# Routing stage: who multiplies the found places by their indices, GpSimd or VectorE

## The chip, the cores and the metric

The kernel runs on one core of a Trainium2 chip, alone. The metric is the device time of one execution in microseconds (us), the median of several. Six parts of the core matter here: TensorE (PE, matrix products; PEld is its weight load), VectorE (DVE), ScalarE (ACT), GpSimd (POOL), SyncE (SP, which issues most DMAs) and the DMA engines. They run side by side and wait for each other on semaphores only.

## What is computed

One decoder layer over 528 rows (16 meta tokens and 512 real ones, width 2048): attention and a recurrence side by side, an output projection, and then PEER, a feed-forward layer that picks experts per token. The change lies in PEER's routing:

```python
q = (xt @ w_q).reshape(T, PEER_HEADS, 2, PEER_DHALF)
s = jnp.einsum('thcd,hcnd->thcn', q, sub_keys).astype(jnp.float32)
s1v, s1i = lax.top_k(s[:, :, 0], PEER_TOPK)
s2v, s2i = lax.top_k(s[:, :, 1], PEER_TOPK)
cand = (s1v[..., :, None] + s2v[..., None, :]).reshape(T, PEER_HEADS, PEER_TOPK * PEER_TOPK)
cidx = (s1i[..., :, None] * PEER_NKEYS + s2i[..., None, :]).reshape(T, PEER_HEADS, PEER_TOPK * PEER_TOPK)
top_s, top_pos = lax.top_k(cand, PEER_TOPK)
eidx = jnp.take_along_axis(cidx, top_pos, axis=-1)
gates = jax.nn.softmax(top_s, axis=-1)
```

For each of 8 heads and 512 tokens there are two rows of 128 scores. The 16 best of each are taken with their indices, 16 of the sums of pairs are kept, and the two indices of each kept pair name the expert. The `take_along_axis` is the part that the change touches.

## The kernel before, in words

**Stages.** The layer is a chain of blocks: norm, input projection, attention, recurrence, output projection, norm, routing (`route`, some 1040 to 1290 us of the profiled execution), a table of gates (`gate_table`, to some 1480 us) and the experts (`experts`, to the end at 3562 us). Each engine has its own instruction stream in a block.

**The weights' stream.** The routing projects the normed rows with w_q, one piece of 256 columns for each head m. A piece has four steps g. For each step SP loads a raw tile, ACT rounds it to a high part (L298, `split_high`), and POOL subtracts to get the low part (L312, `split_low`, called a split below). PE takes both parts (L343 to L345, 24 matmuls per step) when the low part is there. There are two buffers of high and low parts, so the split of step g can start only when PE has released step g - 2.

**A head on its way.** After step 0 of piece m, PE makes the scores of head m - 1 (L1423), ACT copies them to SBUF (L1456), and VectorE works on head m - 1. VectorE's head is this list:

- the search over the scores: maxima (L1501), places of the maxima (L1505), removal of them (L1508), and the same again for the next eight
- a cast of the found indices to float (L1528) and the sums of pairs (L1534)
- the same search over the sums
- sixteen numbers per token kept (L1543), bit operations on the places (L1545 to L1548), a cast (L1549), and arithmetic on them (L1550 to L1554)
- `keep` of the head before (two reductions, L1517), which waits for `hot_done`
- two comparisons (L1559, one for each half) that write `route_hot`, a tile of ones and zeros: 4 token blocks x 16 kept pairs x 16 ranks per partition, 1024 elements

**Who multiplies.** `route_hot` is multiplied by the float indices (`route_idx_f`), and the sum over the ranks (`keep`) then is the index of the kept pair. Before, POOL multiplies: `weigh`, two instructions of 128x1024 (L1396). In POOL's stream `weigh(m, s)` stands between the splits of steps 1 and 2 of piece m and works on head m - 2, since it waits until `places_met` has reached m - 1. The last two heads' multiplications stand behind the last split. `route_hot`, `route_idx_f` and the scores have two slots each, for even and odd heads.

**The end of the stage.** Behind head 7 VectorE subtracts the top score (L1579, L1580), ACT takes the exponential, VectorE keeps the last head (L1517) and scales the gates (L1584 to L1586). PE then transposes the picks for the table (L1633).

Of the kernel before, what the change touches and what calls it, by code (L numbers as in the profile page):

```python
# [24 lines left out]
ALU = mybir.AluOpType  # L25
# [7 lines left out]
P = 128  # L33
# [3 lines left out]
TB = T // P  # L37
# [14 lines left out]
PH, NK, TOPK = 8, 128, 16  # L52
# [7 lines left out]
class Count:  # L60
# [10 lines left out]
    def link(self, ins):  # L71

        self.up(ins)
        self.wait()
# [599 lines left out]
def pl(start, count):  # L674
    return bass.ds(start, count)
# [670 lines left out]
def route(nc, place, kb, stream, xT, picks, cst, plain_stored):  # L1346


    with ExitStack() as ctx:
        def sem(name):  # L1350
            return ctx.enter_context(nc.semaphore(f"route_{name}"))
# [6 lines left out]
        hot = place("route_hot", [P, 2, 2, TB, TOPK, TOPK], F32, kb + 20)  # L1358
        val = place("route_val", [P, 2, TB, TOPK], F32, kb + 36)
        idx = place("route_idx", [P, 2, TB, TOPK], U32, kb + 36.5)  # L1360
        idx_f = place("route_idx_f", [P, 2, 2, TB, TOPK], F32, kb + 37)
# [9 lines left out]
        places_met, hot_done, waited = sem("places_met"), sem("hot_done"), sem("waited")  # L1371
# [6 lines left out]
        def each_head(eng, head, peeled):  # L1378

            for m in range(peeled):  # L1380
                head(m, m % 2, True)
            with eng.Fori(peeled // 2, PH // 2) as i:
                for s in range(2):
                    head(i * 2 + s, s, False)

        @block.sync
        def _(sp):
            stream.load_rest(sp, PH)

        @block.gpsimd  # L1390
        def _(pool):
            def weigh(m, s):

                pool.wait_ge(places_met, m - 1)
                for c in range(2):
                    last = pool.tensor_tensor(  # L1396
                        hot[:, s, c], hot[:, s, c],
                        idx_f[:, s, c].unsqueeze(2).to_broadcast([P, TB, TOPK, TOPK]), ALU.mult)
                last.then_inc(hot_done, 1)

            def head(m, s, first):
                for g in range(QSTEPS):
                    if not (first and m == 0 and g < 2):
                        stream.split_low(pool, m, g)
                    if g == 1 and not first:
                        weigh(m, s)

            each_head(pool, head, 2)
            weigh(PH, 0)
            weigh(PH + 1, 1)  # L1410

        @block.tensor
        def _(pe):
# [72 lines left out]
        def _(dve):  # L1486
# [3 lines left out]
            def take_wait():  # L1490

                dve.sem_inc(waited, 1)

            def top16(rows, rests, values, places):

                take_wait()
                for part in range(2):
# [12 lines left out]
                    link(last)  # L1510
                    take_wait()

            def keep(m, s):

                dve.wait_ge(hot_done, m)
                for c in range(2):
                    last = dve.tensor_reduce(picks[c][:, :, pl(m * TOPK - TOPK, TOPK)], hot[:, s, c],  # L1517
                                             AX.X, ALU.add)
                link(last)

            def head(m, s, first):
# [9 lines left out]
                for ranks, width, at in ((slice(0, WIDE), TOPK, 0),  # L1531
                                         (slice(WIDE, TOPK), NARROW, WIDE * TOPK)):
                    rows = ranks.stop - ranks.start
                    last = dve.tensor_tensor(  # L1534
                        cand[:, :, at:at + rows * width].rearrange("p b (i j) -> p b i j", j=width),
                        val[:, 0, :, ranks].unsqueeze(3).to_broadcast([P, TB, rows, width]),
                        val[:, 1, :, 0:width].unsqueeze(2).to_broadcast([P, TB, rows, width]),
                        ALU.add)
# [16 lines left out]
                if not (first and m == 0):  # L1555
                    keep(m, 1 - s)

                for c in range(2):
                    last = dve.tensor_tensor(  # L1559
                        hot[:, s, c].rearrange("p b n r -> p (b n) r"),  # L1560
                        pos_f[:, c].rearrange("p b n -> p (b n)").unsqueeze(2)
                        .to_broadcast([P, TB * TOPK, TOPK]),
                        cst["iota"][:, 0:TOPK].unsqueeze(1).to_broadcast([P, TB * TOPK, TOPK]),
                        ALU.is_equal)
                last.then_inc(places_met, 1)

            dve.wait_ge(plain_stored, 16)
            head(0, 0, True)
            head(1, 1, True)
            with dve.Fori(1, PH // 2) as i:  # L1570
                count.enter(i - 1, 2 * HEAD_LINKS)
                for s in range(2):
                    head(i * 2 + s, s, False)
                count.leave(PH // 2 - 1)
# [5 lines left out]
            dve.tensor_tensor(gates, gates, tops.unsqueeze(3).to_broadcast([P, TB, PH, TOPK]),  # L1580
                              ALU.subtract).then_inc(shifted, 1)
            keep(PH, 1)
            dve.wait_ge(exp_done, 1)
            link(dve.tensor_reduce(total[:, 1], gates, AX.X, ALU.add))  # L1584
# [651 lines left out]
```

## Time and profile before

| | us |
|---|---|
| median of 3 runs | 3577.05 |
| lowest, highest | 3573.82, 3586.83 |
| the profiled execution | 3564.46 |
| its span on the core | 3562.6 |
| PE busy | 3357.4 (94%) |
| DVE busy | 2235.9 (63%) |
| ACT busy | 1118.1 (31%) |
| POOL busy | 1162.3 (33%) |

The profile is of one execution. Its span runs from the first to the last instruction, and some 2 us lie around it. Busy time is a mean over stages with different limits: in the experts, the last two thirds, PE is never idle, while in the routing it has idle time. A row in order of time gives start, length, engine, line, operation and shapes, and in brackets how long the engine had been idle and what ended that. The length of an instruction includes time in which it stood on the engine and could not proceed.

### The profile page before, as it was taken

The numbers are of one execution on the slowest core, as the hardware profiler recorded it, in microseconds if no ns is written. First come the engines' busy times: TensorE is split into PE (matmuls) and PEld (weight loads), VectorE is DVE, ScalarE is ACT, GpSimd is POOL, SyncE is SP. The second block draws the span as 40 slices with busy tenths as digits, with TensorE's granted clock in tenths as the row PEclk, the third lists the DMA queues.
The fourth block names the chain that finished last, engine by engine and source line by source line (L and its number), as shares of the span: only waits on it lengthen the run. The fifth ranks groups of instructions, "written<-read, shape, count | busy, mean of one in ns | idle before, by whom it ended". The sixth has DMA issues, their size and how long they took to land.

```text
span 3562.6 us, 51459 instructions
## 1 busy us (share of the span) xinstructions
PE 3357.4 (94%) x16926; PEld 2941.1 (83%) x16926; DVE 2235.9 (63%) x3877; ACT 1118.1 (31%) x1732; POOL 1162.3 (33%) x870
## 2 busy tenths in 40 slices
PE   7999999777989947899999999999999999999999
PEld 5778876666868746799998998998998998998998
DVE  2003412794027899667777777777777777777676
ACT  3122223443232249332233223232233222222222
POOL 2344431263435510322322322323323333333332
PEclk9999999899999979999999999999999999999999
DMA  4233320003322124887887888887888888888876
GB/s 140 74 86 95 96 80 20 1 1 118 95 105 83 59 83 188 298 265 262 275 263 260 275 261 264 269 267 259 273 265 263 271 265 264 269 266 263 269 263 233
DMA packets 276020, 686.84 MB, mean 193 GB/s; under 512 B 120544, under 2 KB 120800, under 8 KB 273504
## 3 DMA queue, kind: packets, MB, share of 16 engines
q1 hardware_dynamic: 202224, 417.51, 36.2%
q0 software_dynamic: 73728, 268.47, 22.5%
q8 instruction: 37, 0.61, 0.1%
q14 instruction: 31, 0.25, 0.0%
HBM read 655.48 MB, written 30.41 MB: 193 GB/s over the span
## 4 chain that ended last, share of the span: by engine, by line
PE 59%; ACT 2%; issue 1%; DMA 1%; ACTq 0%; DVE 0%; DVEq 0%; SPq 0%
PE exp_a L1864 10%; PE exp_a L1866 10%; PE exp_a L1865 10%; PE exp_o L1885 10%; PE exp_o L1887 10%; PE exp_o L1883 10%; ACT table_gaps L1682 1%; ACT table_stage L1698 1%; DMA gate_table<-table_stage 0%; PE table_b L1642 0%; ACTq L1682 0%; DMA exp_raw<-in_v 0%; ACTq L1698 0%; PE table_t L1633 0%; DVE table_hot L1668 0%
## 5 line engine op out<-in xcount | busy, mean ns | idle before, releaser
L1864 PE MATMUL exp_a<-x_high,exp_uh 128*128 128x384 f32 x2048 | 686.3, 335 | 10.0 <-DVE exp_ul L1948 10.0
L1866 PE MATMUL exp_a<-x_high,exp_ul 128*128 128x384 f32 x2048 | 685.8, 335 | 0.0
L1865 PE MATMUL exp_a<-x_low,exp_uh 128*128 128x384 f32 x2048 | 685.7, 335 | 0.0
L1887 PE MATMUL exp_o<-exp_vh,exp_al 128*128 128x512 f32 x1536 | 598.2, 389 | 0.0
L1885 PE MATMUL exp_o<-exp_vl,exp_ah 128*128 128x512 f32 x1536 | 598.1, 389 | 0.0
L1883 PE MATMUL exp_o<-exp_vh,exp_ah 128*128 128x512 f32 x1536 | 597.5, 389 | 0.0
L1843 POOL DMA_INDIRECT exp_rows<-in_v_rows,exp_now x256 | 326.8, 1277 | 710.1 <-DVE h L1969 658.6
L1843 POOL DMA_INDIRECT exp_rows<-in_u_rows,exp_now x256 | 299.9, 1171 | 732.1 <-DVE exp_rows L1962 687.1
L1913 ACT CAST exp_vh<-exp_raw 128x1024 fp32r<-128x1024 f32 x256 | 260.0, 1050 | 516.5 <-PE exp_o L1887 493.2
L1948 DVE TENSOR_TENSOR exp_vl<-exp_raw,exp_vh 128x1024 fp32r<-128x1024 f32 x256 | 304.6, 1220 | 164.7 <-ACT exp_vh L1913 164.7
L1864 PEld LDWEIGHTS exp_a<-x_high,exp_uh 128*128 128x128 f32 x2048 | 385.6, 188 | 11.7 <-DVE exp_ul L1948 7.3
L1865 PEld LDWEIGHTS exp_a<-x_low,exp_uh 128*128 128x128 f32 x2048 | 385.6, 188 | 1.2
L1866 PEld LDWEIGHTS exp_a<-x_high,exp_ul 128*128 128x128 f32 x2048 | 385.5, 188 | 0.0
L1924 ACT ACTIVATE exp_act<-exp_a 128x384 f32<-128x384 f32 x128 | 63.0, 492 | 962.3 <-PE exp_a L1866 962.3
L1887 PEld LDWEIGHTS exp_o<-exp_vh,exp_al 128*128 128x128 f32 x1536 | 288.3, 188 | 60.0
L1885 PEld LDWEIGHTS exp_o<-exp_vl,exp_ah 128*128 128x128 f32 x1536 | 288.3, 188 | 59.3
L1883 PEld LDWEIGHTS exp_o<-exp_vh,exp_ah 128*128 128x128 f32 x1536 | 288.3, 188 | 59.2
L1948 DVE TENSOR_TENSOR exp_ul<-exp_raw,exp_uh 128x1024 fp32r<-128x1024 f32 x256 | 309.8, 1221 | 41.5 <-ACT exp_uh L1913 31.5
L312 POOL TENSOR_TENSOR w_in_lo<-w_in_raw,w_in_hi 128x1024 fp32r<-128x1024 f32 x88 | 212.9, 2419 | 332.6 <-ACT w_in_hi L298 332.6
L1969 DVE SCALAR_TENSOR_TENSOR h<-exp_rows,exp_weights,h 128x1024 f32<-128x1024 f32 x256 | 316.5, 1277 | 0.0
L1962 DVE SCALAR_TENSOR_TENSOR exp_rows<-exp_rows,sparse_x 128x1024 f32<-128x1024 f32 x256 | 302.4, 1218 | 0.0
L1989 DVE TENSOR_TENSOR exp_act<-exp_act,exp_gates 128x384 f32<-128x384 f32 x128 | 71.9, 562 | 360.3 <-ACT exp_act L1924 360.3
(290 smaller groups left out, 5182.0 us busy)
## 6 DMA issues: line engine op xcount, KB each, us to landing
exp_raw<-in_u SPq DMA_DIRECT2D x256, 512.0 KB, 5.3
exp_raw<-in_v SPq DMA_DIRECT2D x256, 512.0 KB, 4.4
w_in_raw<-in_w_in SPq DMA_DIRECT2D x88, 512.0 KB, 3.6
gate_table<-table_stage SPq DMA_DIRECT2D x6, 4096.0 KB, 11.6
exp_gates<-gate_table SPq DMA_DIRECT2D x128, 192.0 KB, 5.3
w_out_raw<-in_w_out SPq DMA_DIRECT2D x32, 512.0 KB, 3.7
w_q_raw<-in_w_q SPq DMA_DIRECT2D x32, 512.0 KB, 3.9
x_rows<-in_x SPq DMA_DIRECT2D x4, 1024.0 KB, 8.3
```

The lines of the kernel that those rows point to most:

```text
L312: eng.tensor_tensor(self.lo[:, g % 2], self.raw[:, g % RAW], self.hi[:, g % 2].bitcast(F32), ALU.subtract).then_inc(self.low, 1)
L1843: pool.indirect_dma_start(rows[slot][:, :], None, sparse["u" if kind == "dot" else "v"], bass.IndirectOffsetOnAxis(ap=now[:, turn, place_n ...
L1864: pe.matmul(bank, uh[:, b, c, :], xh[:, 0:DENSE_TB, c, :], start=(c == 0), stop=False)
L1865: pe.matmul(bank, uh[:, b, c, :], xl[:, 0:DENSE_TB, c, :], start=False, stop=False)
L1866: last = pe.matmul(bank, ul[:, b, c, :], xh[:, 0:DENSE_TB, c, :], start=False, stop=(c == DC - 1))
L1883: pe.matmul(bank[:, :], ah[:, key, tokens], vh[:, dc % 2, key, :], start=(key == 0), stop=False)
L1885: pe.matmul(bank[:, :], ah[:, key, tokens], vl[:, dc % 2, key, :], start=False, stop=False)
L1887: last = pe.matmul(bank[:, :], al[:, key, tokens], vh[:, dc % 2, key, :], start=False, stop=(key == KEYS_OF_MACRO - 1))
L1913: act.copy(part(uh if split[0] == "u" else vh, *split, half), raw[:, c % RAW_SLOTS, :])\
L1948: dve.tensor_tensor(part(ul if kind == "u" else vl, kind, which, half), raw[:, slot, :], part(uh if kind == "u" else vh, kind, which, half ...
L1962: done = dve.scalar_tensor_tensor(rows[slot][:, :], rows[slot][:, :], 1.0, sparse["x"][:, half, :], ALU.mult, ALU.mult, accum_out=dots[:, ...
L1969: done = dve.scalar_tensor_tensor(sums, rows[slot][:, :], weights[:, pl(pick(m, kind, t), 1)], sums, ALU.mult, ALU.add)
```

## The change

POOL's function `weigh` and its calls go, and its stream in this stage holds the splits alone. VectorE gets a function `weigh(s)` with the same two instructions on the same operands. It is called at the end of each head, behind the two comparisons and a wait for them on `places_met`. The semaphore `hot_done` is raised by VectorE now, one head earlier in order than before, and `keep` still waits for it.

```diff
--- before.py
+++ after.py
@@ -1389,25 +1389,12 @@
 
         @block.gpsimd
         def _(pool):
-            def weigh(m, s):
-
-                pool.wait_ge(places_met, m - 1)
-                for c in range(2):
-                    last = pool.tensor_tensor(
-                        hot[:, s, c], hot[:, s, c],
-                        idx_f[:, s, c].unsqueeze(2).to_broadcast([P, TB, TOPK, TOPK]), ALU.mult)
-                last.then_inc(hot_done, 1)
-
             def head(m, s, first):
                 for g in range(QSTEPS):
                     if not (first and m == 0 and g < 2):
                         stream.split_low(pool, m, g)
-                    if g == 1 and not first:
-                        weigh(m, s)
 
             each_head(pool, head, 2)
-            weigh(PH, 0)
-            weigh(PH + 1, 1)
 
         @block.tensor
         def _(pe):
@@ -1510,6 +1497,14 @@
                     link(last)
                     take_wait()
 
+            def weigh(s):
+
+                for c in range(2):
+                    last = dve.tensor_tensor(
+                        hot[:, s, c], hot[:, s, c],
+                        idx_f[:, s, c].unsqueeze(2).to_broadcast([P, TB, TOPK, TOPK]), ALU.mult)
+                last.then_inc(hot_done, 1)
+
             def keep(m, s):
 
                 dve.wait_ge(hot_done, m)
@@ -1563,6 +1558,8 @@
                         cst["iota"][:, 0:TOPK].unsqueeze(1).to_broadcast([P, TB * TOPK, TOPK]),
                         ALU.is_equal)
                 last.then_inc(places_met, 1)
+                dve.wait_ge(places_met, m + 1)
+                weigh(s)
 
             dve.wait_ge(plain_stored, 16)
             head(0, 0, True)
```

POOL's stream in the routing, the first part of the loop's body. `w_q_lo` is the low part of a step, `route_hot` the tile that is multiplied. Before:

```order
L312 TENSOR_TENSOR w_q_lo<-w_q_raw,w_q_hi 128x1024
L1394 REGISTER_ALU
L1396 TENSOR_TENSOR route_hot<-route_hot,route_idx_f 128x1024 x2
L311 REGISTER_ALU
L312 TENSOR_TENSOR w_q_lo<-w_q_raw,w_q_hi 128x1024
L311 REGISTER_ALU
L312 TENSOR_TENSOR w_q_lo<-w_q_raw,w_q_hi 128x1024
L311 ISA
L312 TENSOR_TENSOR w_q_lo<-w_q_raw,w_q_hi 128x1024
L311 REGISTER_ALU
```

And now:

```order
L312 TENSOR_TENSOR w_q_lo<-w_q_raw,w_q_hi 128x1024
L311 REGISTER_ALU
L312 TENSOR_TENSOR w_q_lo<-w_q_raw,w_q_hi 128x1024
L311 REGISTER_ALU
L312 TENSOR_TENSOR w_q_lo<-w_q_raw,w_q_hi 128x1024
L311 ISA
L312 TENSOR_TENSOR w_q_lo<-w_q_raw,w_q_hi 128x1024
L311 REGISTER_ALU
L312 TENSOR_TENSOR w_q_lo<-w_q_raw,w_q_hi 128x1024
```

The pair of multiplications between the second and third split is gone, and the splits stand in a row.

VectorE's stream, the end of the second head in the loop's body and what stands behind the loop. `picks` are the kept indices. Before:

```order
L1554 TENSOR_TENSOR route_pos_f<-route_pos_f,route_quarterf 128x64
L77 REGISTER_ALU
L1517 ISA
L1517 TENSOR_REDUCE picks_77<-route_hot 128x4x16
L1517 REGISTER_ALU
L1517 TENSOR_REDUCE picks_78<-route_hot 128x4x16
L77 REGISTER_ALU
L1559 TENSOR_TENSOR route_hot<-route_pos_f,c_iota 128x1024 x2
L1570 REGISTER_ALU
L1570 COMPARE_AND_BRANCH
L1579 COPY route_total<-picks_79 128x32
L1580 TENSOR_TENSOR picks_79<-picks_79,route_total 128x512
L1517 TENSOR_REDUCE picks_77<-route_hot 128x4x16
```

And now:

```order
L1512 ISA
L1512 TENSOR_REDUCE picks_77<-route_hot 128x4x16
L1512 REGISTER_ALU
L1512 TENSOR_REDUCE picks_78<-route_hot 128x4x16
L77 REGISTER_ALU
L1554 TENSOR_TENSOR route_hot<-route_pos_f,c_iota 128x1024 x2
L1561 REGISTER_ALU
L1503 TENSOR_TENSOR route_hot<-route_hot,route_idx_f 128x1024 x2
L1567 REGISTER_ALU
L1567 COMPARE_AND_BRANCH
L1576 COPY route_total<-picks_79 128x32
L1577 TENSOR_TENSOR picks_79<-picks_79,route_total 128x512
L1512 TENSOR_REDUCE picks_77<-route_hot 128x4x16
```

Behind the two comparisons there is now a pair of multiplications, ahead of the branch that ends the loop's body, so every head's search starts behind the multiplications of the head before it.

## Rows read from the trace of the kernel before

**Rows 1.** A stretch of the experts: busy us (instructions) of PE, PEld, DVE, ACT, POOL, clock, DMA.
```profile
1500.00:3500.00 2000.00, 2000.00 (x10186) 1828.67 (x10185) 1477.61 (x1824) 577.16 (x727) 631.78 (x546) 1.00 0.81 267
```

**Rows 2.** The waits of 1040 to 1300 us: sum, times, longest.
```profile
DVE route_val L1501 <- ACT route_scores L1456: 39.2, 6, 32.1
...
PE route_q L343 <- POOL w_q_lo L312: 9.1, 6, 3.6
```

**Rows 3.** VectorE in order of time, the stage's end: start, length, idle before.
```profile
1281.13 0.18 DVE L1579 COPY route_total<-picks 128x32 f32<-128x32 f32 x1
1281.35 2.83 DVE L1580 TENSOR_TENSOR picks<-picks,route_total 128x512 f32<-128x512 f32 x1
1286.41 2.35 DVE L1517 TENSOR_REDUCE picks<-route_hot 128x64 f32<-128x1024 f32 x2 [2.23 <-POOL route_hot L1396]
1288.79 0.69 DVE L1584 TENSOR_REDUCE route_total<-picks 128x32 f32<-128x512 f32 x1
```

**Rows 4.** VectorE in order of time, head 6 and the start of head 7.
```profile
1234.48 0.30 DVE L1501 MAX8 route_val<-route_scores 128x8 f32<-128x128 f32 x1 [1.73 <-ACT route_scores L1456]
...
1245.06 0.69 DVE L1534 TENSOR_TENSOR route_cand<-route_val 128x256 f32<-128x256 f32 x2
...
1251.42 0.19 DVE L1545 TENSOR_SCALAR route_pos<-route_pos 128x64 uint32<-128x64 uint32 x1
...
1253.16 2.35 DVE L1517 TENSOR_REDUCE picks<-route_hot 128x1024 f32 x2
1255.54 2.36 DVE L1559 TENSOR_TENSOR route_hot<-route_pos_f,c_iota 128x1024 f32<-128x1024 f32 x2
1257.82 0.29 DVE L1501 MAX8 route_val<-route_scores 128x8 f32<-128x128 f32 x1
```

**Rows 5.** Groups of 1040 to 1300 us: busy, mean ns | idle before, releaser.
```profile
L1396 POOL TENSOR_TENSOR route_hot<-route_hot,route_idx_f 128x1024 f32<-128x1024 f32 x16 | 38.2, 2410 | 51.9 <-DVE route_hot L1559 51.9
L1559 DVE TENSOR_TENSOR route_hot<-route_pos_f,c_iota 128x1024 f32<-128x1024 f32 x16 | 21.4, 1378 | 0.3
...
L1549 DVE CAST route_quarterf<-route_pos 128x256 f32<-128x256 uint32 x8 | 4.5, 559 | 0.3
L1554 DVE TENSOR_TENSOR route_pos_f<-route_pos_f,route_quarterf 128x64 f32<-128x64 f32 x8 | 3.9, 484 | 0.3
L1545 DVE TENSOR_SCALAR route_pos<-route_pos 128x64 uint32<-128x64 uint32 x8 | 3.7, 464 | 0.0
```

**Rows 6.** VectorE and GpSimd in order of time, where both are at work.
```profile
1097.78 2.40 POOL L312 TENSOR_TENSOR w_q_lo<-w_q_raw,w_q_hi 128x1024 fp32r<-128x1024 f32 x1 [3.47 <-ACT w_q_hi L298]
1097.91 2.41 DVE L1549 CAST route_quarterf<-route_pos 128x256 f32<-128x256 uint32 x1
...
1228.01 1.22 DVE L1517 TENSOR_REDUCE picks<-route_hot 128x1024 f32 x1
1228.13 2.40 POOL L312 TENSOR_TENSOR w_q_lo<-w_q_raw,w_q_hi 128x1024 fp32r<-128x1024 f32 x1 [3.47 <-ACT w_q_hi L298]
```

**Rows 7.** GpSimd and VectorE in order of time, the norm before the routing.
```profile
1029.57 3.33 POOL L312 TENSOR_TENSOR w_q_lo<-w_q_raw,w_q_hi 128x1024 fp32r<-128x1024 f32 x1
1030.62 3.37 DVE L206 TENSOR_SCALAR scaled_rows<-h,ffnnorm_stat 128x2048 f32<-128x2048 f32 x1
```

**Rows 8.** VectorE in order of time, its first work in the routing.
```profile
1080.55 1.65 DVE L1501 MAX8 route_val<-route_scores 128x8 f32<-128x128 f32 x8 [32.10 <-ACT route_scores L1456]
```

**Rows 9.** GpSimd in order of time: the four splits of piece 1, first of 2.
```profile
1068.35 2.39 POOL L312 TENSOR_TENSOR w_q_lo<-w_q_raw,w_q_hi 128x1024 fp32r<-128x1024 f32 x1 [3.05 <-ACT w_q_hi L298]
1074.22 2.40 POOL L312 TENSOR_TENSOR w_q_lo<-w_q_raw,w_q_hi 128x1024 fp32r<-128x1024 f32 x1 [3.48 <-ACT w_q_hi L298]
1079.23 2.40 POOL L312 TENSOR_TENSOR w_q_lo<-w_q_raw,w_q_hi 128x1024 fp32r<-128x1024 f32 x1 [2.61 <-ACT w_q_hi L298]
1086.47 2.40 POOL L312 TENSOR_TENSOR w_q_lo<-w_q_raw,w_q_hi 128x1024 fp32r<-128x1024 f32 x1 [4.84 <-ACT w_q_hi L298]
1091.91 2.40 POOL L312 TENSOR_TENSOR w_q_lo<-w_q_raw,w_q_hi 128x1024 fp32r<-128x1024 f32 x1 [3.04 <-ACT w_q_hi L298]
```

## What the change does to the time, predicted

> **What bounds the kernel now.** I read the page's busy times first, then the waits of the routing stage, then VectorE in order of time through it, and then VectorE and GpSimd side by side.
>
> The experts, the last two thirds, are bound by TensorE: in 2000 us it is busy for 2000.00 at a clock of 1.00 [rows 1]. The change doesn't touch them. What it can do is to move the moment at which they begin, and that moment hangs on the routing's last step. The table of gates starts from VectorE's last sums, which begin at 1288.79 [rows 3], and nothing of the table can start earlier, because its transposes need the picks of all heads.
>
> Within the routing two engines take turns as the bound. VectorE begins head 0 at 1080.55 [rows 8]. Until 1288.79 that is 208.24 us, and I split it:
>
> - An undisturbed head is 1257.82 - 1234.48 = 23.34 us [rows 4]. Head 0 has no keep, which is 1255.54 - 1253.16 = 2.38 less: 20.96. Eight heads are 20.96 + 7 x 23.34 = 184.3.
> - The end: 0.22 for L1579, 0.69 for L1580 if it runs alone (L1584 works on as many elements in 0.69), 2.38 for the two L1517: 3.3 [rows 3, 4].
> - Waits for scores: 39.2 in six waits, 32.1 of them ahead of head 0, so 7.1 [rows 2]. These are TensorE's: it waits 9.1 us for late low parts, in front of which GpSimd's multiplications stand.
> - The wait for GpSimd's last multiplications, 2.23, and L1580 held up by them, 2.83 - 0.69 = 2.1 [rows 3].
> - VectorE standing still beside a split. L1549 issued at 1097.91 takes 2.41, just as long as a split that began at 1097.78 [rows 6]; the other seven take 4.5 - 2.4 = 2.1, or 0.3 each. From the groups [rows 5]: 2.1 in L1549, 8 x (464 - 190) ns = 2.2 in L1545, about 2.1 in L1554 at an undisturbed 0.22, and 16 x (1378 - 1220) ns = 2.5 in L1559. Together 8.9.
>
> The sum is 184.3 + 3.3 + 7.1 + 2.2 + 2.1 + 8.9 = 207.9, against 208.2 measured. The account closes, so VectorE is at its limit for 187.6 of 208 us, and any work that is put on it lies on the path.
>
> **What the change takes away.** GpSimd loses 16 instructions, 38.2 us [rows 5]. They weren't on the path as such; what goes is what they caused: the waits for scores (7.1, since VectorE will be the later one, below), the last wait (2.2) and the hold-up of L1580 (2.1). That is 11.4 us.
>
> **What it adds.** VectorE gets 16 instructions on 1024 elements with two SBUF inputs, the form of L1559. A pair of L1559 takes 1257.82 - 1255.54 = 2.28 from its start to the next instruction [rows 4]. The new wait on its own comparison costs the overlap of two instructions, 1.22 - 1.14, and a little for the semaphore: 0.1, an estimate. So 2.4 per head, and a head is 25.74. Undisturbed: 20.96 + 2.4 + 7 x 25.74 + 3.3 = 206.8, or 1.4 less than now. Nothing but that wait is queued behind it: next on VectorE is the search of the next head, which waits with it.
>
> **What is late next.** GpSimd's splits of piece m come at 1068.35, 1074.22, 1079.23 and 1086.47 plus 23.56 x (m - 1), since 1091.91 - 1068.35 = 23.56 is a piece with no multiplication in it [rows 9]. The scores of head m are then ready at 1080.5 + 23.56 m, those of head 7 at 1245.4. VectorE at 25.74 and more per head never waits for them again, and a split that comes a little late costs nothing. But VectorE also loses its step with TensorE: it drifts by over 2 us per head against the splits, and can no longer stay clear of them as head 6 does now, where nothing exceeds its undisturbed length [rows 4].
>
> **The price of meeting a split.** Three things are read from rows. A VectorE instruction that is issued while a split runs waits until it is over (L1549) [rows 6]. A reduction doesn't: L1517 takes 1.22 beside a split of 2.40 [rows 6]. And where both are queued without a pause they alternate: a split issued at 1029.57 lasts 3.33, to 1032.90, because L206 goes first, and the next L206, issued at 1030.62, lasts 3.37 and so gets through only behind it [rows 7]. So a split that comes due within a chain of VectorE's instructions costs VectorE its full length, about 2.35, and one that already runs costs the rest. In a head such chains are L1528 and L1534 (some 0.8 us, at +10.3), L1543 to L1554 (at +16.8 to +18.5), L1559 (at +21.05 to +23.3), and now the multiplications (to +25.7): the last chain doubles [rows 4]. GpSimd's own multiplications met none of them: they started right behind L1559 (all 51.9 us of idle before them end with it [rows 5]) and ran beside the search, which does not stop for GpSimd.
>
> The Trainium skill ("SBUF — State Buffer", section "Who interferes with whom") names the cause: a VectorE instruction with two SBUF inputs shares a read interface with a GpSimd instruction that reads SBUF, and who issues first holds it for the whole instruction. It doesn't say who is next when both are queued. If VectorE kept it through a chain, the second rival below would hold; the rows above show turns.
>
> **The walk.** I step through the heads with these offsets and the splits' times:
>
> | head | starts | stalls | next starts |
> |---|---|---|---|
> | 0 | 1080.55 | 2.4 in L1549 (there before too), 2.3 at the multiplications (split due 1102.8) | 1108.5 |
> | 1 | 1108.5 | 2.3 in L1552 (1126.35), 2.3 at the multiplications (1133.6) | 1138.9 |
> | 2 | 1138.9 | 2.3 in L1554 (1157.15), 2.4 between the multiplications (1162.6) | 1169.3 |
> | 3 | 1169.3 | 2.4 in L1543 (1186.15), 1.6 in L1559 (1192.0), 2.4 between the multiplications (1197.0) | 1201.5 |
> | 4 | 1201.5 | 0.3 in L1528 (1209.7), 0.1 in L1559 (1220.6) | 1227.7 |
> | 5 | 1227.7 | none, the last split is at 1227.8 | 1253.4 |
> | 6, 7 | 1253.4 | none | 1304.9 |
>
> The stalls sum to 20.9. Undisturbed 206.8 + 20.9 = 227.7, against 208.2: **19.4 us later**. One meeting is a matter of 0.05 us, L1554 at 1157.2 in head 2; without it, and with what shifts behind it, I get 17.0. I take the middle, **18 us**.
>
> All of it should arrive at the end: behind the routing comes a table stage whose engines start together, and then a TensorE without a gap [rows 1]. TensorE's clock is not part of the sum, as it idles for tens of us ahead of the table in both.
>
> **The rivals.**
>
> *Turns that fall well, or a VectorE that keeps its port* (stalls as now). Only a split already at work stops VectorE. Then the stalls are about the 8.9 of today: 206.8 + 8.9 - 208.2 = +7.5 us. For it: head 6 of now shows no stall at all [rows 4]. Against it: the turns of [rows 7], and that this head was in step with TensorE, for whose scores it had waited 1.73.
>
> *Every split of the overlap meets a chain.* In heads 0 to 4 some 24 splits pass, and a head could meet 3 rather than 2 of them: 2 to 5 more meetings of 2.35 on top of the walk's 19.4, or +24 to +31 us. A piece that is itself slowed by late splits would prolong the overlap and lead here.
>
> *Not slower.* The multiplications slip between splits, since ScalarE's rounding, ahead of each split, shifts with TensorE, and the chain ends before a split is due. It decides if fewer than one meeting in all is left: 206.8 - 208.2 = -1.4 us, at best. With head 0's stall, which the change doesn't touch, +1. The 11.4 us won pay for the 19.2 of new work (8 x 2.4) only together with the stalls of 8.9. A gain over 0.5% has no row for it.
>
> **How the numbers follow.** The profiled execution took 3564.46, which is 12.6 below the median of the runs shown, and within it the routing's place is read to 0.1 us; the difference is the same on either, so I add it to the median: 3577.05 + 18 = **3595.0**. Chances: the walk (+16 to +21) 0.56, well-fallen turns (+4 to +12) 0.22, more meetings (+24 to +31) 0.14, not slower (-3 to +3) 0.08. What a measurement of this kernel can tell from no change is about 0.5%, or 17.9 us, and my forecast lies on that line: I give half of the walk to either side. Slower by over 0.5%: 0.28 + 0.14 = 0.42, and a little for losses that no row shows, 0.45; faster 0.02; the same 0.53. The range leaves out the not slower and most of the case of more meetings: 3580 to 3602.
>
> **What would show it right or wrong.** In the profile of the changed kernel: 16 multiplications on VectorE at a mean over 1.6 us though the shortest take 1.21; waits of VectorE for scores only ahead of head 0; TensorE's 9.1 us of waits for splits down to some 1; its last product of this stage some 12 us earlier than now; heads 5 to 7 at 25.7 us each; and the last sums (now L1584, 1288.79) at some 1307. The step most likely to fail is the count of meetings: if L1554 and the multiplications keep their undisturbed 0.23 and 1.21, the second or fourth case holds. If the last sums come late and the end doesn't, the table stage has given it back.

## The result

| | before | changed |
|---|---|---|
| median of 20 runs, us | 3575.92 | 3586.71 |
| lowest, highest | 3560.89, 3587.51 | 3575.90, 3595.77 |
| span of the profiled execution | 3562.6 | 3593.9 |
| first search of the routing to last sums | 208.2 | 224.5 |

The changed kernel takes 1.0031 times as long, with a 95% interval of 1.0019 to 1.0043: 10.8 us more, between 7 and 15. That is slower, and by less than 0.5%.

### The profile page after: what moved, and what is told of

It is laid out like the page before. It is cut to its first block, busy times and chain, and to the rows that moved or that the text cites. A ratio compares the mean times of both kernels' runs of the same rounds, so it can differ in the third digit from the quotient of the medians.

```text
span 3593.9 us, 51462 instructions
## 1 busy us (share of the span) xinstructions
PE 3366.5 (94%) x16926; PEld 2951.7 (82%) x16926; DVE 2260.8 (63%) x3893; ACT 1118.1 (31%) x1732; POOL 1132.0 (31%) x854
## 4 chain that ended last, share of the span: by engine, by line
PE 59%; ACT 2%; issue 1%; DMA 1%; DVE 0%; ACTq 0%; DVEq 0%; SPq 0%
PE exp_a L1861 10%; PE exp_a L1863 10%; PE exp_a L1862 10%; PE exp_o L1882 10%; PE exp_o L1884 10%; PE exp_o L1880 10%; ACT table_gaps L1679 1%; ACT table_stage L1695 1%; DMA gate_table<-table_stage 0%; PE table_b L1639 0%; DMA exp_raw<-in_v 0%; ACTq L1679 0%; DVE table_hot L1665 0%; ACTq L1695 0%; PE table_t L1630 0%
## 5 line engine op out<-in xcount | busy, mean ns | idle before, releaser
L1945 DVE TENSOR_TENSOR exp_vl<-exp_raw,exp_vh 128x1024 fp32r<-128x1024 f32 x256 | 304.5, 1220 | 164.7 <-ACT exp_vh L1910 164.7
L1945 DVE TENSOR_TENSOR exp_ul<-exp_raw,exp_uh 128x1024 fp32r<-128x1024 f32 x256 | 309.7, 1220 | 41.6 <-ACT exp_uh L1910 31.6
```

Of the source, the lines that this page charges most:

```text
L1945: dve.tensor_tensor(part(ul if kind == "u" else vl, kind, which, half), raw[:, slot, :], part(uh if kind == "u" else vh, kind, which, half ...
```

## The profile of the changed kernel

The two profiled spans differ by 31.3 us, three times the medians' difference, so I looked first at where this lies. These are stretches of the changed kernel, with the columns of [rows 1]:

```profile
600.00:900.00 300.00, 238.81 (x1332) 202.56 (x1332) 207.62 (x409) 116.21 (x290) 105.84 (x128) 0.83 0.10 34
1160.00:1185.00 25.00, 25.00 (x121) 20.97 (x120) 23.44 (x88) 7.74 (x10) 10.51 (x4) 1.00 0.30 92
1500.00:3500.00 2000.00, 2000.00 (x10184) 1828.24 (x10183) 1476.83 (x1829) 580.79 (x731) 630.83 (x546) 1.00 0.81 267
```

And two of them in the kernel before:

```profile
600.00:900.00 300.00, 239.06 (x1405) 202.45 (x1406) 209.83 (x412) 120.88 (x298) 112.80 (x131) 0.90 0.11 39
1160.00:1185.00 25.00, 22.19 (x94) 18.43 (x95) 21.58 (x87) 5.69 (x8) 11.94 (x6) 0.86 0.28 85
```

In the 300 us of attention and recurrence, where the change touches nothing, the granted clock was 0.83 in the one execution and 0.90 in the other. The routing's first search is at 1097.31 and not at 1080.55 [rows 8], 16.8 us of the 31.3. The experts are the same in both, 2000.00 of 2000 us busy. From the last sums to the end it is 2272.1 us, and 2273.8 before. So I compare the routing alone, from VectorE's first search to its last sums (L1584 before [rows 3], L1581 now): 16.2 us more. The second stretch will be needed below: TensorE runs in it at a clock of 1.00 without a gap now (and so in all of 1100 to 1250 us), and at 0.86, with 2.81 us idle, in the stretch of before that has the same times.

The end of the stage on VectorE, in order of time, answers to [rows 3]:

```profile
1316.29 2.36 DVE L1503 TENSOR_TENSOR route_hot<-route_hot,route_idx_f 128x1024 f32<-128x1024 f32 x2
1318.57 0.18 DVE L1576 COPY route_total<-picks 128x32 f32<-128x32 f32 x1
1318.78 0.69 DVE L1577 TENSOR_TENSOR picks<-picks,route_total 128x512 f32<-128x512 f32 x1
1319.39 2.34 DVE L1512 TENSOR_REDUCE picks<-route_hot 128x64 f32<-128x1024 f32 x2
1321.76 0.69 DVE L1581 TENSOR_REDUCE route_total<-picks 128x32 f32<-128x512 f32 x1
```

The last comparison is followed by the multiplications at once, L1577 takes 0.69 and not 2.83, and the wait for GpSimd is gone. From L1576 to the last sums it takes 3.19 us, before 7.66.

The groups of the routing, in the columns of [rows 5]:

```profile
L1554 DVE TENSOR_TENSOR route_hot<-route_pos_f,c_iota 128x1024 f32<-128x1024 f32 x16 | 24.0, 1538 | 0.3
L1503 DVE TENSOR_TENSOR route_hot<-route_hot,route_idx_f 128x1024 f32<-128x1024 f32 x16 | 23.1, 1487 | 0.3
...
L1538 DVE COPY picks<-route_best 128x64 f32 x6 | 5.8, 962 | 1.4 <-DVE route_pos L1492 1.4
...
L1544 DVE CAST route_quarterf<-route_pos 128x256 f32<-128x256 uint32 x8 | 4.5, 558 | 0.3
L1523 DVE CAST route_idx_f<-route_idx 128x128 f32<-128x128 uint32 x8 | 3.8, 480 | 1.9 <-DVE route_idx L1492 1.9
...
L1549 DVE TENSOR_TENSOR route_pos_f<-route_pos_f,route_quarterf 128x64 f32<-128x64 f32 x8 | 1.8, 225 | 0.3
L1540 DVE TENSOR_SCALAR route_pos<-route_pos 128x64 uint32<-128x64 uint32 x8 | 1.5, 184 | 0.0
```

Each multiplication takes 1487 ns in the mean and each comparison 1538, while an undisturbed one takes 1.22. The cast L1544 has its one long instruction as before, L1549 and L1540 have none now. L1523 has one, and the copy L1538 has three: they take 1.89, 1.04 and 2.25 us where an undisturbed one takes 0.19. VectorE waited for scores ahead of head 0 alone, and TensorE waited for no split at all.

Head 6 starts at 1267.17 and head 7 at 1292.87:

```profile
1267.17 1.64 DVE L1488 MAX8 route_val<-route_scores 128x8 f32<-128x128 f32 x8
...
1292.87 0.86 DVE L1488 MAX8 route_val<-route_scores 128x8 f32<-128x128 f32 x4
```

That is 25.70 us for a head that meets no split, where it was 23.34 [rows 4]. All eight take 27.33, 25.77, 29.61, 29.83, 31.62, 25.70, 25.70 and 25.7 us. Over an undisturbed 23.3 (head 0) and 25.7, the stalls are 4.0, 0, 3.9, 4.1, 5.9, 0, 0 and 0, together 17.9. Counted by instruction, ten stand beside a split and last 18.2 us longer in all than undisturbed ones.

## Experiment 1: how much the routing differs between executions

Both kernels again, with no edit. The second profile of before:

> The kernel before, unchanged, to see how much the routing itself differs between executions. I measure it from VectorE's first search (head 0) to its last sums (L1584): 208.2 us in the profile of before, 224.5 in the profile of after. Theory (the loss is made inside the routing by work on VectorE and by its meetings with GpSimd's splits, both of which repeat): 207 to 210 again, and any other difference in the span lies ahead of the routing. Rival (the difference of the two profiles, 16.2 us, is partly chance, since the medians differ by 10.8 only): the length comes out several us longer, 211 to 215.

It took **213.2 us**. And of the changed kernel:

> The changed kernel, unchanged. Theory: 224 to 225 us from first search to last sums, with the same stalls in the same heads (head 1 and heads 5 to 7 none). Rival (meetings are drawn anew in each execution): another pattern and a length between 216 and 226, on average nearer to 219, which would explain a median difference of 10.8.

It took **224.5 us**, and each of its heads is within 0.04 us of the first profile's. The changed routing repeats; the routing before doesn't. The reason is in head 4. This is the first profile of before, VectorE and GpSimd in order of time:

```profile
1202.96 0.23 DVE L1554 TENSOR_TENSOR route_pos_f<-route_pos_f,route_quarterf 128x64 f32<-128x64 f32 x1
1202.99 2.46 POOL L312 TENSOR_TENSOR w_q_lo<-w_q_raw,w_q_hi 128x1024 fp32r<-128x1024 f32 x1 [3.46 <-ACT w_q_hi L298]
```

And this the second (its times are 5.0 us less at the same place), with GpSimd's multiplications and TensorE's next wait below:

```profile
1197.99 2.40 POOL L312 TENSOR_TENSOR w_q_lo<-w_q_raw,w_q_hi 128x1024 fp32r<-128x1024 f32 x1 [3.46 <-ACT w_q_hi L298]
1198.02 2.44 DVE L1554 TENSOR_TENSOR route_pos_f<-route_pos_f,route_quarterf 128x64 f32<-128x64 f32 x1
...
1205.42 4.75 POOL L1396 TENSOR_TENSOR route_hot<-route_hot,route_idx_f 128x1024 f32<-128x1024 f32 x2 [5.04 <-DVE route_hot L1559]
1212.53 0.79 PE L343 MATMUL route_q<-x_high,w_q_hi 128*128 128x512 f32 x1 [3.51 <-POOL w_q_lo L312]
```

In the first, L1554 is issued 0.03 us ahead of the split, takes 0.23, and the split starts with it. In the second it is issued 0.03 us behind and stands for 2.44. Then everything behind it is late in turn: the comparisons, GpSimd's multiplications that wait for them, the split behind those, and TensorE, which waits 3.51 us for it. Its first matmul then takes 0.79 and the next ones 0.63, where they took 0.39 ahead of the wait, since the granted clock is at the lower of its two levels there, 1.2 of 2.4 GHz (columns of [rows 1]):

```profile
1212.00:1218.00 6.00, 5.47 (x13) 4.31 (x14) 5.32 (x33) 0.00 (x0) 2.80 (x2) 0.50 0.50 154
```

So the wait costs TensorE more than its own length. The stretch of before shown above, at a clock of 0.86, holds such a wait too (the longest of [rows 2]). A meeting of 0.03 us cost 5 us.

Two more profiles of before, the second with the count of the common case in mind:

> The kernel before, unchanged, a third profile. Its routing was 208.2 us in the first and 213.2 in the second, and the two part at one place: in head 4 VectorE's L1554 was issued 0.03 us ahead of a split in the one and 0.03 us behind one in the other. Theory (a near tie with two outcomes): 208.2 or 213.2 us, nothing between, and 29.1 us for head 5 in the second case. Rival (a drift with many outcomes): some other length.

> The kernel before, unchanged, a fourth profile. Theory: 208.2 or 213.2 us. If 213 is the common case, then the changed kernel's 224.5 is 11.3 us more than a usual run of before, which is the 10.8 us by which the medians differ. Rival: 208 is common, and 5 us of the difference of the profiles is given back somewhere that I haven't found.

They took **208.8** and **207.2 us**. So two outcomes was too simple: head 1 took 27.4 us in both of them and 25.8 in the first two, and heads 3 and 5 vary too. (The second profile is from another chip than the third and fourth; how much of the variation is the chip's isn't separated.) The four profiles have a mean of 209.4, and the changed kernel is 15.1 us above that.

## Experiment 2: where GpSimd multiplies

The edit to the kernel before:

```diff
-                    if g == 1 and not first:
+                    if g == 2 and not first:
                         weigh(m, s)
```

> The kernel before with GpSimd's two multiplications behind the third split of a piece and not behind the second. GpSimd idles 4.84 us there and 2.6 behind the second. Theory (before the change, the only harm of the multiplications was that they made the third split late, which held TensorE and so the scores): TensorE's waits for splits fall from 9.1 us to under 2, VectorE's waits for scores shrink, the routing takes about 199 us and the kernel is 9 us faster than before, ratio 0.9975. Rival (the multiplications' place doesn't matter, because VectorE's own 184 us and its meetings bind): the same as before, 206 to 210 us, ratio 1.000.

Measured: **ratio 0.9967** (0.9948 to 0.9986), and 201.7 us in the routing. The waits that remain are these, for splits and for scores, in the columns of [rows 2]:

```profile
PE route_q L343 <- POOL w_q_lo L312: 2.1, 5, 0.4
DVE route_val L1501 <- ACT route_scores L1456: 32.7, 2, 32.1
```

TensorE's 9.1 us went to 2.1, and of VectorE's waits for scores only 0.6 are left beside the one ahead of head 0. So the place of the multiplications in GpSimd's stream was worth 7.7 us of the routing, with no work moved.

## Experiment 3: half of the multiplications on each engine

On top of that edit, VectorE multiplies half 0 behind its comparisons, and GpSimd's `weigh` has half 1 alone, behind the third split:

```diff
                 last.then_inc(places_met, 1)
+                dve.wait_ge(places_met, m + 1)
+                dve.tensor_tensor(
+                    hot[:, s, 0], hot[:, s, 0],
+                    idx_f[:, s, 0].unsqueeze(2).to_broadcast([P, TB, TOPK, TOPK]), ALU.mult)\
+                    .then_inc(hot_done, 1)
...
-                dve.wait_ge(hot_done, m)
+                dve.wait_ge(hot_done, m * 2)
```

> One of the two multiplications of a head on VectorE, the other on GpSimd behind the third split. Theory: half of the new work (8 x 1.25 = 10 us) and some 11 us of stalls: 209 us for the routing, the same as before, ratio 1.000, and so half of the way from weigh_late to the changed kernel. Rival (the loss comes from the drift against the splits and not from the amount of work): nearer to the changed kernel, 218 us or more, ratio 1.003.

Measured: **ratio 0.9990** (0.9972 to 1.0007), 209.8 us in the routing. It lies 8.1 us above `weigh_late` and 14.6 below the changed kernel. So the amount of work counts, and drift against the splits alone does not decide. The interval holds 1: this kernel can't be told from before.

## Experiment 4: what a meeting costs

The splits of this stage on half of the tile:

```diff
-                        stream.split_low(pool, m, g)
+                        pool.wait_ge(stream.high, m * stream.steps + (g + 1))
+                        pool.tensor_tensor(stream.lo[:, g % 2, 0:QSPAN // 2], stream.raw[:, g % RAW, 0:QSPAN // 2],
+                                           stream.hi[:, g % 2, 0:QSPAN // 2].bitcast(F32),
+                                           ALU.subtract).then_inc(stream.low, 1)
```

> The changed kernel, but each of GpSimd's splits of w_q in this stage works on half of the tile (the low parts' other half is stale), so that it takes 1.2 us and not 2.4. VectorE's work is that of the changed kernel. Theory (VectorE stands still while a split runs): stalls fall from 17.9 us to about 9, routing 215 to 216 us. Rival (VectorE's longer instructions have another cause, and only their number counts): 224 us.

Measured: **215.2 us**. The shorter splits and the multiplications, in the columns of [rows 5]:

```profile
L1396 POOL TENSOR_TENSOR w_q_lo<-w_q_raw,w_q_hi 128x512 fp32r<-128x512 f32 x30 | 41.4, 1380 | 146.6 <-ACT w_q_hi L298 146.6
L1506 DVE TENSOR_TENSOR route_hot<-route_hot,route_idx_f 128x1024 f32<-128x1024 f32 x16 | 21.1, 1358 | 0.3
```

VectorE's instructions are those of the changed kernel, and TensorE waits for no split in either. In both kernels ten instructions stand beside a split. They lose 18.2 us in the changed kernel and 9.1 here: as many meetings, each half as long, and the routing is 9.3 us shorter. That is the cause shown: VectorE stands still while a split runs. (This kernel, the next one and `double` ran once each; they have a profile and no interval.)

The other way round, the multiplications' places filled with reductions of the same tile, so that the picks are wrong:

```diff
-                    last = dve.tensor_tensor(
-                        hot[:, s, c], hot[:, s, c],
-                        idx_f[:, s, c].unsqueeze(2).to_broadcast([P, TB, TOPK, TOPK]), ALU.mult)
+                    last = dve.tensor_reduce(pos_f[:, c], hot[:, s, c], AX.X, ALU.add)
```

> The changed kernel with the 16 multiplications replaced by 16 reductions of the same tile, as long as them but with one input (the picks are then sums of ones). Theory (only an instruction with two inputs from SBUF, a copy, a cast or the like waits for GpSimd): none of the 16 takes over 1.25 us, though splits run beside them, while the comparisons and small steps before them still stall, 12 to 16 us in all at another alignment: routing 219 to 223 us. Rival (any work of VectorE is held up by a split): reductions of up to 3.5 us and 224 us.

Measured: **222.2 us**. The comparisons, with two inputs, and the 16 new reductions:

```profile
L1552 DVE TENSOR_TENSOR route_hot<-route_pos_f,c_iota 128x1024 f32<-128x1024 f32 x16 | 24.4, 1564 | 0.3
L1503 DVE TENSOR_REDUCE route_pos_f<-route_hot 128x64 f32<-128x1024 f32 x16 | 18.8, 1214 | 0.3
```

None of the reductions was held up (the longest took 1.22), while the comparisons in front of them took 1564 ns in the mean. The Trainium skill says so of this chip ("SBUF — State Buffer", section "Who interferes with whom"): a `tensor_reduce` never contends with GpSimd. The trace agrees: 7 of the 16 ran beside a split, and none of these was longer than 1.22. It isn't one input that makes the difference, as the copy L1538 and the cast L1523 of the changed kernel have one too and were held up. It saved only 2.2 us of the 224.5, though. The multiplications' own stalls had been 16 x (1487 - 1220) ns = 4.3 us, and half of that came back at other instructions, since the splits come anyway.

## Experiment 5: twice the multiplications

```diff
+                for c in range(2):
+                    last = dve.tensor_tensor(hot[:, s, c], hot[:, s, c], hot[:, s, c], ALU.mult)
+                last.then_inc(hot_doubled, 1)
+                dve.wait_ge(hot_doubled, m + 1)
                 for c in range(2):
```

> The changed kernel with each tile of ones and zeros also multiplied by itself first, which changes no value: 16 more instructions of the same form on VectorE. Theory: 8 x 2.4 = 19.2 us of new work and 4 to 7 us more stalls, since the chain in which a split can come due is 2.4 us longer: routing 248 to 251 us. Rival (work alone): 243.7 us.

Measured: **249.3 us**, 24.8 above the changed kernel. Its heads 5, 6 and 7, behind the last split, take 28.1 us where they took 25.7, which is 2.4 of work each; 8 x 2.4 = 19.2 are work, and 5.6 are stalls. The rival of work alone (243.7) is out.

## Experiment 6: no multiplications at all

The function `weigh` raises the semaphore only, and leaves the products out:

```diff
-                for c in range(2):
-                    last = dve.tensor_tensor(
-                        hot[:, s, c], hot[:, s, c],
-                        idx_f[:, s, c].unsqueeze(2).to_broadcast([P, TB, TOPK, TOPK]), ALU.mult)
-                last.then_inc(hot_done, 1)
+                dve.sem_inc(hot_done, 1)
```

> The changed kernel without the multiplications on either engine (left out: the picks are then sums of ones, so the experts chosen are wrong). Theory: VectorE's head falls back to 23.34 us, below the 23.56 that a piece takes TensorE, so it is held in step by the scores again. Routing 195 to 198 us (changed kernel: 224.5), with two or three stalls left, 7 to 9 us in all; ratio to the kernel before 0.995 or so. The multiplications on VectorE then cost 224.5 - 196 = 28 us: 19.2 of work, the rest stalls that come with them. Rival (the stalls belong to the search and its small steps and not to the longer chain): 224.5 - 19.2 = 205 us.

Measured: **ratio 1.0008** (0.9987 to 1.0030), and 209.3 us. My expectation missed by 11 to 14 us: a kernel without the 16 instructions on any engine is no faster than the one with them on GpSimd. The head starts showed a pause that I had not counted, in the brackets of the first search of head 3:

```profile
1165.47 1.65 DVE L1488 MAX8 route_val<-route_scores 128x8 f32<-128x128 f32 x8 [0.36 <-DVE route_hot L1550]
```

The wait and the semaphore step, with nothing in between to hide them, cost 0.4 to 0.8 us in each head from the second on. So the undisturbed head was 23.9 and not 23.3 us, longer than TensorE's 23.56. To tell the pause from the small steps themselves, the same once more without it:

```diff
-                dve.wait_ge(hot_done, m)
+                dve.wait_ge(places_met, m)
...
                 last.then_inc(places_met, 1)
-                dve.wait_ge(places_met, m + 1)
-                weigh(s)
```

> The kernel without the multiplications (left out, the picks are sums of ones), now also without the semaphore step that stood in their place in the run before: keep waits for places_met directly, so VectorE's head has no pause at its end. Theory (what made that run 209 us was its 0.4 to 0.8 us pause per head, which took VectorE out of step with TensorE, and the meetings that followed): an undisturbed head is 23.34 us, below TensorE's 23.56, and the routing 195 to 199 us, ratio 0.996. Rival (the small steps meet splits with no multiplication in play, pause or no pause): 203 to 209 us, ratio 0.999.

Measured: **ratio 0.9961** (0.9943 to 0.9979), and 194.4 us. The pauses sum to 3.3 us and their removal gave 14.9. Its heads 2 to 5 take 23.58, 23.55, 23.56 and 23.56 us, TensorE's pace to 0.02 us, without a wait for scores. What holds the pace is this, in head 3 (VectorE's rows and GpSimd's, in order of time):

```profile
1187.59 2.35 DVE L1512 TENSOR_REDUCE picks<-route_hot 128x1024 f32 x2
1187.92 2.40 POOL L312 TENSOR_TENSOR w_q_lo<-w_q_raw,w_q_hi 128x1024 fp32r<-128x1024 f32 x1 [2.61 <-ACT w_q_hi L298]
1189.97 2.57 DVE L1554 TENSOR_TENSOR route_hot<-route_pos_f,c_iota 128x1024 f32<-128x1024 f32 x2
1192.46 0.28 DVE L1488 MAX8 route_val<-route_scores 128x8 f32<-128x128 f32 x1
```

The comparisons stand for the last 0.2 us of a split (2.57 against 2.36) in heads 3, 4 and 5; in head 2 they don't, and its 0.2 us lie elsewhere. VectorE, which would be 0.22 us faster, runs up against the same split in each of the three and is put back by just that. I read this as being locked to TensorE's step through the splits, clear of all other meetings. With 0.5 us more per head VectorE is slower than TensorE and slides along the splits: eight instructions are held up in heads 1 to 4 of `no_multiply`, and two in those of `no_multiply_lean` beside the 0.2 us in heads 3 and 4.

## Experiment 7: a version that beats both

`weigh_late`, and the last head's multiplications on VectorE, where no split runs any more and GpSimd's would be waited for:

```diff
-            weigh(PH + 1, 1)
...
+            dve.wait_ge(places_met, PH)
+            for c in range(2):
+                last = dve.tensor_tensor(
+                    hot[:, 1, c], hot[:, 1, c],
+                    idx_f[:, 1, c].unsqueeze(2).to_broadcast([P, TB, TOPK, TOPK]), ALU.mult)
+            last.then_inc(hot_done, 1)
```

> GpSimd multiplies behind the third split, as in weigh_late (routing 201.7 us, ratio 0.9967), but the last head's two multiplications are VectorE's. In weigh_late the end from the last comparison took 7.66 us as before: L1580 held up by GpSimd and a wait for it of 2.2. Theory: both go for 2.4 us of work, so 5.6 us in place of 7.6, the routing 199.7 us, and faster than before by 0.3 to 0.4%. Rival (the end is hidden by the exponential on ScalarE): 201.7 us.

Measured: **ratio 0.9970** (0.9955 to 0.9984), and 199.6 us. The end of the stage:

```profile
1279.51 2.36 DVE L1577 TENSOR_TENSOR route_hot<-route_hot,route_idx_f 128x1024 f32<-128x1024 f32 x2
1282.01 0.69 DVE L1584 TENSOR_TENSOR picks<-picks,route_total 128x512 f32<-128x512 f32 x1
1282.62 2.34 DVE L1516 TENSOR_REDUCE picks<-route_hot 128x64 f32<-128x1024 f32 x2
1284.99 0.69 DVE L1588 TENSOR_REDUCE route_total<-picks 128x32 f32<-128x512 f32 x1
```

From the multiplications to the last sums it is 5.48 us, where from L1579 alone it was 7.66 [rows 3]. The 2 us are plain at the end of the routing, which took 7.66 in all four profiles of before and in `weigh_late`, and too small for the ratio, which can't tell this version from `weigh_late`. Against the changed kernel it takes 24.9 us less in the routing.

All runs in one table. The expected times are those of the prediction's walk for the changed kernel and those that I wrote down ahead of each run for the others. The difference is to the 209.4 of before, and 1 us is 0.00028 of the ratio. A ratio and an interval need several executions; the kernels without them ran once:

| kernel | expected, us | routing, us | against 209.4 | ratio (interval) |
|---|---|---|---|---|
| before, four profiles | 208 | 208.2, 213.2, 208.8, 207.2 | | |
| changed, two profiles | 225 to 228 | 224.5, 224.5 | +15.1 | 1.0031 (1.0019 to 1.0043) |
| weigh_late | 199 | 201.7 | -7.7 | 0.9967 (0.9948 to 0.9986) |
| halves | 209 | 209.8 | +0.4 | 0.9990 (0.9972 to 1.0007) |
| no_multiply | 195 to 198 | 209.3 | -0.1 | 1.0008 (0.9987 to 1.0030) |
| no_multiply_lean | 195 to 199 | 194.4 | -15.0 | 0.9961 (0.9943 to 0.9979) |
| late_tail | 199.7 | 199.6 | -9.8 | 0.9970 (0.9955 to 0.9984) |
| splits_half | 215 to 216 | 215.2 | +5.8 | |
| reduce_instead | 219 to 223 | 222.2 | +12.8 | |
| double | 248 to 251 | 249.3 | +39.9 | |

## Why the prediction came out as it did

**Right: the direction, the place and the mechanism.** VectorE is the bound of the routing, an undisturbed head is 25.70 us (forecast 25.74), GpSimd's relief is worth what was read for it (the end 4.5 us shorter, no wait for scores, none for splits), and the rest is stalls. Undisturbed, the routing comes to 224.5 - 17.9 = 206.6 us against the forecast 206.8. The range held the time, and the price of a meeting holds as well: what is left of the split, from 0.85 to 2.20 us. One sentence at the top of this text is too narrow for it: engines don't wait for each other on semaphores only, as an instruction that stands beside a split waits on none.

**Too big: the stalls, 20.9 forecast and 17.9 measured.** The step that failed is the walk in head 1, where I had two meetings and there was none. Both were missed by hundredths. This is head 0, in which a split was due while the comparisons ran:

```profile
1119.54 2.96 POOL L312 TENSOR_TENSOR w_q_lo<-w_q_raw,w_q_hi 128x1024 fp32r<-128x1024 f32 x1 [2.61 <-ACT w_q_hi L298]
1120.28 4.43 DVE L1503 TENSOR_TENSOR route_hot<-route_hot,route_idx_f 128x1024 f32<-128x1024 f32 x2
```

The split lasts 2.96 from its issue, so it began its own work 0.57 later, and the multiplications stood for 2.07 (4.43 against 2.36), not for my 2.35. Head 1 began 0.6 us earlier in its step for that, and then:

```profile
1143.10 2.48 POOL L312 TENSOR_TENSOR w_q_lo<-w_q_raw,w_q_hi 128x1024 fp32r<-128x1024 f32 x1 [2.61 <-ACT w_q_hi L298]
1143.10 0.23 DVE L1549 TENSOR_TENSOR route_pos_f<-route_pos_f,route_quarterf 128x64 f32<-128x64 f32 x1
...
1148.14 2.36 DVE L1503 TENSOR_TENSOR route_hot<-route_hot,route_idx_f 128x1024 f32<-128x1024 f32 x2
1150.35 2.41 POOL L312 TENSOR_TENSOR w_q_lo<-w_q_raw,w_q_hi 128x1024 fp32r<-128x1024 f32 x1 [4.76 <-ACT w_q_hi L298]
```

L1549 is issued at the same 1143.10 as the split and goes first, and the last split is due at 1150.35, with the multiplications' end at 1150.5: it lasts 2.41, so it lost nothing by them. I had called head 2's meeting a matter of 0.05 us and taken the middle for that one alone, while each of the walk's eleven meetings had the same doubt. Heads 2, 3 and 4 had 13.9 us of stalls, where the walk had 11.5. That the sum came so near is partly luck: five of its eleven meetings came at the instruction where the walk had them, and only head 0's two of these with about its length. Head 4 had 5.9 us of stalls and not 0.4, and head 1's 4.6 us too many were set against that.

**Too small: the time of before.** I took 208.2 us as the routing of before. Four profiles give 207.2 to 213.2 and a mean of 209.4, so 1.2 us of the loss isn't one. Together, 3.0 for the stalls, 1.2 for the base and 0.2 for the undisturbed sum make 19.4 into 15.1 (to 0.1, by rounding).

**What stays open: 15.1 us in the profiles, 10.8 in the medians.** The interval reaches to 15.4, so the two agree, though at its edge. In time, 3595.0 was 8.3 us above the measured 3586.7: 1.1 is the median of before, 3577.05 from three runs and 3575.92 from twenty, and 7.2 are 18 against 10.8. Nothing behind the routing gives time back: from the last sums to the end the four profiles of before have 2273.8, 2272.4, 2273.8 and 2274.6 us, the two of the changed kernel 2272.1 and 2274.1. That the common run of before has a longer routing than my four profiles is possible, as one of them had 213.2, which is 11.3 below the 224.5; it isn't shown. The stretch ahead of the routing alone varies by more than 10 us.

**The rivals.** *Turns that fall well* (+7.5 us; the prediction also calls it the second rival) is nearer to the medians' 10.8 than the walk's 17.0 to 19.4 is, but its mechanism is refuted: VectorE doesn't keep its place through a chain, a split gets in between. Head 4 of the changed kernel shows it, where the two multiplications follow each other without a wait:

```profile
1236.99 4.56 DVE L1503 TENSOR_TENSOR route_hot<-route_hot,route_idx_f 128x1024 f32<-128x1024 f32 x2
1237.34 3.12 POOL L312 TENSOR_TENSOR w_q_lo<-w_q_raw,w_q_hi 128x1024 fp32r<-128x1024 f32 x1 [2.61 <-ACT w_q_hi L298]
```

The split is issued within the first multiplication and lasts 3.12, so it goes ahead of the second, and the pair takes 4.56 and not 2.36. And the changed routing was longer than each of the four of before, by 11 to 17 us. *More meetings* and *not slower* did not come. I had counted the relief of TensorE as worth nothing beyond its 7.1 us; in `weigh_late` this relief is all that the edit aims at, and it is worth 7.7.

**The expected signs.** The multiplications' mean was 1.49 us and not over 1.6, TensorE's waits for splits 0 and not 1. TensorE's idle time ahead of the table grew from 37.9 to 67.7 us, of which 16.2 are the later table and 13.6 its earlier end (forecast 12).

## What to carry to other kernels

Where VectorE and GpSimd share a stage, walk VectorE's instructions with two SBUF inputs, its copies and its casts in time against GpSimd's work, and trust the sum more than the place of a single meeting: the walk came within 3.2 us of the measured stage for the changed kernel, the times expected ahead of the runs did for seven of the eight other kernels, and the one miss was a pause of 0.5 us per head that I hadn't counted. Before moving work off an engine, look for a gap in its own stream, since GpSimd idled 4.84 us [rows 9] one position behind the place where its 4.75 us of multiplications made TensorE wait. And take more than one profile of the kernel before, since its stage differed by 6 us over four executions, while the changed one's heads repeated to 0.04 in two.

## What the runs showed that I had not expected

- A meeting won or lost by 0.03 us changed the stage by 5 us, since the late split behind it let TensorE wait 3.5 us, and the granted clock was 0.50 in the 6 us behind that wait.
- Sixteen instructions fewer in all gave nothing (ratio 1.0008), until a pause was gone too (0.9961) that, at 3.3 us in all, was a sixth of their 19.2 us on VectorE.
- An engine a little faster than the one it follows can lock to its pace through such meetings (heads of 23.56 us, where 23.34 was possible), and one a little slower slides through more of them: 0.5 us per head made 15 us of the stage. The 15 us are measured; the locking is read from three heads of one profile.
- The reduction was not held up beside a split (7 of 7 at 1.21 to 1.22 us), while copies and casts with one input were. But putting it in the multiplications' place saved 2.2 us only, as half of the stalls came back at other instructions.
